# A two-layer hybrid diffusion backbone on one core: the attention loop visits the two latent query chunks first and the context chunk last

## The reference, cut to what matters

```python
def one_block(qblk):                       # 128 queries, all heads
    s = jnp.einsum('bqhd,bkhd->bhqk', qblk, k).astype(jnp.float32) * scale
    p = jax.nn.softmax(s, axis=-1)
    return jnp.einsum('bhqk,bkhd->bqhd', p.astype(v.dtype), v)
# context layer: k, v of its 128 tokens; latent layer:
ckv_all = jnp.concatenate([ctx_kv[0], ckv], axis=1)      # 128 cached + 256 latent keys
...
mix = jnp.concatenate([y_ssd, y_ret, y_mla], axis=-1)    # 512 + 256 + 256 columns
x = x + g1 * (mix @ lp['w_out'])
```

## Time and profile before

| | us |
|---|---|
| median of 3 runs (lowest, highest) | 1055.86 (1054.91, 1057.27) |
| the profiled execution | 1055.28 |
| its span, first to last instruction | 1053.5 |
| PE busy in the span | 1026.3 (97%) |
| DVE busy | 633.6 (60%) |
| ACT busy | 439.5 (42%) |
| share of PE in the chain that ended last | 93% |

### The profile page before, as it was taken

How to read it: one execution, slowest core, us unless ns; L and a number is a source line. 1 busy time by engine, 2 the same in 40 slices (tenths; PEclk the granted TensorE clock), 3 DMA queues, 4 the chain that set the end, 5 groups by cost and what they waited for, 6 DMA issues and landing times.

```text
span 1053.5 us, 16439 instructions
## 1 busy us (share of the span) xinstructions
PE 1026.3 (97%) x6552; PEld 938.3 (89%) x6552; DVE 633.6 (60%) x1134; ACT 439.5 (42%) x684; POOL 104.7 (10%) x99
## 2 busy tenths in 40 slices
PE   7899999999999999999999999999999999999995
PEld 4698995779999989999999999667999999999995
DVE  6686868768555553534448787877765555453333
ACT  3256445446333332343334656644643333333231
POOL 0004323003000000000100223300200000000100
PEclk9999999999999999999999999999999999999998
DMA  9843246214333478333464224451233333633331
GB/s 383 327 167 123 81 160 219 110 46 162 122 128 133 176 282 323 116 111 114 133 242 161 91 103 160 146 201 41 81 126 131 132 129 119 252 110 111 122 125 60
DMA packets 30678, 159.56 MB, mean 151 GB/s; under 512 B 3424, under 2 KB 4384, under 8 KB 19872
## 3 DMA queue, kind: packets, MB, share of 16 engines
q1 hardware_dynamic: 28896, 146.75, 38.5%
q10 hardware_dynamic: 1728, 12.06, 2.7%
HBM read 156.27 MB, written 2.52 MB: 151 GB/s over the span
## 4 chain that ended last, share of the span: by engine, by line
PE 93%; DVE 3%; ACT 2%; ACTq 1%; DMA 1%; issue 0%; POOL 0%; DVEq 0%; POOLq 0%
PE ps L472 26%; PE ps L474 26%; PE ps L473 26%; PE ps L501 3%; PE ps L909 1%; DVE wlo L1349 1%; PE ps L799 1%; PE ps L889 1%; PE ps L716 1%; PE ps L743 1%; DMA adas<-wada_dram 1%; PE ps L568 1%; ACTq L1061 1%; PE ps L820 1%; ACT whi L1011 1%; PE ps L707 0%
## 5 line engine op out<-in xcount | busy, mean ns | idle before, releaser
L472 PE MATMUL ps<-h_hi,whi 128*128 128x386 f32 (+1 forms) x1120 | 384.9, 344 | 0.1
L474 PE MATMUL ps<-h_hi,wlo 128*128 128x386 f32 (+1 forms) x1120 | 379.7, 339 | 0.0
L473 PE MATMUL ps<-h_lo,whi 128*128 128x386 f32 (+1 forms) x1120 | 378.7, 338 | 0.0
L1349 DVE TENSOR_TENSOR wlo<-stage,whi 128x2048 fp32r<-128x2048 f32 (+1 forms) x106 | 223.4, 2107 | 153.4 <-ACT whi L1011 153.4
L1011 ACT ACTIVATE whi<-stage 128x2048 fp32r<-128x2048 f32 (+1 forms) x106 | 185.9, 1754 | 229.1 <-PE ps L474 205.2
L472 PEld LDWEIGHTS ps<-h_hi,whi 128*128 128x128 f32 x1120 | 211.3, 189 | 9.6 <-issue 7.6
L473 PEld LDWEIGHTS ps<-h_lo,whi 128*128 128x128 f32 x1120 | 211.6, 189 | 0.3
L474 PEld LDWEIGHTS ps<-h_hi,wlo 128*128 128x128 f32 x1120 | 210.7, 188 | 0.0
L472 PE MATMUL ps<-hid_hi,whi 128*128 128x384 f32 x352 | 118.3, 336 | 0.0
L474 PE MATMUL ps<-hid_hi,wlo 128*128 128x384 f32 x352 | 118.3, 336 | 0.0
L473 PE MATMUL ps<-hid_lo,whi 128*128 128x384 f32 x352 | 118.3, 336 | 0.0
(11 more groups left out here) (295 smaller groups left out, 1145.3 us busy)
## 6 DMA issues: line engine op xcount, KB each, us to landing
stage<-wf_dram SPq DMA_DIRECT2D x44, 1024.0 KB, 4.7
adas<-wada_dram SPq DMA_DIRECT2D x80, 512.0 KB, 5.9
stage<-wf_dram SPq DMA_DIRECT2D x32, 704.0 KB, 4.0
stage<-win_dram SPq DMA_DIRECT2D x20, 1024.0 KB, 4.8
stage<-wout_dram SPq DMA_DIRECT2D x8, 1024.0 KB, 5.8
adaf<-wada_dram ACTq DMA_DIRECT2D x6, 1024.0 KB, 15.3
small<-small_dram SPq DMA_DIRECT2D x2, 1202.5 KB, 9.3
stage<-win_dram ACTq DMA_DIRECT2D x2, 1024.0 KB, 13.4
```

Of the source, the lines that this page charges most:

```text
L472: mm(out, ah, bh, start=(k == 0), stop=False)
L473: mm(out, ah, bl, start=False, stop=False)
L474: return mm(out, al, bh, start=False, stop=(k == n - 1))
L1349: tt(wlo[:, g % 2, 0:width], stage[:, g % 2, 0:width], whi[:, g % 2, 0:width].bitcast(F32), ALU.subtract)\
```

## The change

One line: the table of units visits chunk 1, then chunk 2, then chunk 0. Nothing is added or removed; the first eight units are now wide and the last four narrow, where before the first four were narrow and the last eight wide.

```diff
 RSTD = 5
 SUMS = KD - 2
-ATT = [(c, h) for c in range(NCH) for h in range(HM)]
+ATT = [(c, h) for c in (1, 2, 0) for h in range(HM)]
 NATT = len(ATT)
```

## The result

| | before | changed |
|---|---|---|
| median of 20 runs each, us | 1056.01 | 1059.60 |
| ratio, 95% interval | | 1.0032, 1.0022 to 1.0043 |
| profiled execution, us | 1055.28 | 1060.87 |
| its span, us | 1053.5 | 1058.8 |
| its mean granted clock | 0.996 | 0.992 |

The changed kernel is slower by 0.32% (0.22 to 0.43), some 3.4 us, where 0.7 was forecast. Its median lies above the forecast's range, which ended at 1059.0. The granted clock is the share of full speed (2.4 GHz) at which TensorE was allowed to run.

The account below looks back on a forecast made before the run. PE was taken to set the pace in steps with an output tile, and a chain through ACT and DVE at the end. +0.36 us per layer, +0.7 for two, on the median gave 1056.6 us, range 1054.4 to 1059.0.

Parts of the forecast that it names:

- The sum: Attention loop, per layer: 3.51 us more in the middle, less 0.91, 1.20 and 1.04 at the end, giving +0.36.
- The last wait: PE's longest wait, ahead of the loop's last value product, during the split of block 3: about 1.5 us.
- The upper bound: Per layer +1.3 us: middle terms 0.3, an unhidden maximum 0.3, slower hand-overs at the end 0.5; +2.6 in all.
- the end stays as long as before: Loop's end: narrow units save only 0.91 us ahead of block 2; +5.2 us in all, 1061.1 us; chance 0.10.
- the middle hides the wide units: Steps 3 to 7: PE has slack, so +3.51 us does not come; about -6.3 us, 1049.6 us; chance 0.05.
- The clock falls: Second half's first eight products or so run at half clock: +3 us per layer, 1062.6 us; chance 0.04.
- The sign named for it: A granted clock under 1.00 between 225 and 240 us would show the forecast wrong.
- The end before, also with gaps, ran at 1.00: Argument against a clock fall: the old loop end had idle gaps on PE, yet its granted clock stayed 1.00.
- The longest single wait would be about 1.5 us: Argument against a clock fall: at the loop's new end PE's longest wait, for the split of block 3, is that short.
- The transfer's wait: In layer 1 a transfer held up PE; the clock stayed 1.00 with PE busy 5.72 of 7.00 us.

Follow-up runs that it names:

- the fillers: Extra unread PE products in the changed kernel, ahead of the waits for copy 11 (6) or the scale of unit 10 (3): alone, 1056.93 and 1057.02 us.
- the filled kernel: The changed kernel with 3 extra unread PE products ahead of the scale of unit 10 and 6 ahead of copy 11: 1056.42 us, ratio 0.9996.
- the old order: The kernel before's unit order; profiled with two idle ACT copies ahead of copy 11 (1061.81 us), or the split of block 3 behind the mixer copies (1055.23 us).

## Why the prediction was wrong

- The sum was right as far as it went. +0.36 us per layer was forecast, +0.31 measured in the loop of layer 0; output tile 0, the score of unit 8, the transpose of unit 10 and the second half came within 0.1 us of their forecast places, counted from the loop's start. The last wait was 1.34 us, forecast as about 1.5. The upper bound was added too low: 0.36 + 0.3 + 0.3 + 0.5 is +1.46 per layer, not +1.3, which would put the range's end at 1059.3, still below the median.
- The rival that the end stays as long as before fell: 6.24 us. So did the one that the middle hides the wide units: no bracket on PE there, and the score of unit 8 came late by the amount forecast.
- The step that failed is "The clock falls", given 0.04. It is what happens in most executions: the clock term was put at nothing in the sum, and seven heads in eight fell. Its price was put at 3 us per layer, for eight products or so; at the 0.18 us between the starts of these products eight take 1.4 us, not 3, but the fall lasted for some fifteen of them (4.97 us in place of 2.70). The heads show 1.3 to 2.8 us, and the whole effect is 3.4 us in place of 0.7 + 6. The sign named for it, a clock under 1.00 between 225 and 240, looked at layer 0 alone; in the first profile it was layer 1 that fell.
- The argument against it was twofold, and both parts were wrong. "The end before, also with gaps, ran at 1.00" took the old end as a like case, though PE's busy time in its last 6 us went from 4.97 to 3.86 by the very change that was being weighed. "The longest single wait would be about 1.5 us" looked at one wait; the fillers show that the gaps of the whole end count, since closing either brings the clock back most of the time. The transfer's wait, which the clock had survived, was no like case either. In ten profiles PE waited 0.40 to 1.36 us for it and the clock stayed at 1.00; in the two where it waited 1.66 and 2.17 it fell. So a single wait as long as the loop's last one (1.34) was survived there, 1.36 us in two profiles, with PE otherwise busy; at the loop's end, where PE's work around the wait is sparse, it was not.
- The rule of the Trainium skill ("TensorE: Matmul & The Clock Gate", "Why this matters for your kernels"), that idle gaps between bursts bring the clock down to half, agrees with these runs in its direction (means of 0.53 to 0.78 over the 6 us behind the gaps, between the two levels of 1.2 and 2.4 GHz). It speaks of a gap; that the gaps of a whole stretch count together is what the fillers show. The prediction named it and gave it too small a chance.
- In the loop, +0.31 twice is 0.6 us, yet the filled kernel is level with the kernel before (0.9984 to 1.0007 holds both). Its mean clock, 0.9960 against 0.9951, suggests that the kernel before now and then loses its clock too. The profiles of the old order show two places for that outside the loop's end, the start of the program and the transfer in layer 1; why the filled kernel should lose less there is not shown, and the interval allows for no difference.

## What to carry to other kernels

When work for PE is moved out of a stretch in which it already waits, ask not only whether the wait ends later, but what the clock does in the dense stretch behind it: here the end of the loop got 2.3 us shorter, and the head behind it lost 1.3 to 2.8 us. Compare PE's busy time over the whole sparse stretch before and after, and check several executions, since one head with a clock of 1.00 proves nothing. If the sparse stretch can't be filled with useful work, products that nobody reads can fill the wait; here they made the loop no longer (39.89 us with and without them). Better still is to move what makes PE wait, here a weight split of 1.8 us that stood ahead of the last copy; its block is first used by the fifth tile of the second half, about 8 us behind the loop.

## What was not expected of the hardware

The clock fell at ends of the loop where no single wait of PE was longer than 1.34 us, while it held through a single wait of 1.36 us for the transfer, where PE was otherwise busy. Nine products per layer that nobody reads made the kernel 3 us faster.
